# Attention in another order of units: heads two units later, turns behind the heads, a maximum for each map, and four unread products in the second layer

## The reference

```python
def diff_attend(q, k, v, lam):
    s = jnp.einsum('bqhmd,bkhmd->bhmqk', q, k).astype(jnp.float32) * (DA_QK ** -0.5)
    p = jax.nn.softmax(s, axis=-1)
    a = p[:, :, 0] - lam * p[:, :, 1]
    return jnp.einsum('bhqk,bkhv->bqhv', a.astype(v.dtype), v)

def mla_attend(q_nope, q_rope, k_nope, k_rope, v):
    s = (jnp.einsum('bqhd,bkhd->bhqk', q_nope, k_nope)
         + jnp.einsum('bqhr,bkr->bhqk', q_rope, k_rope)).astype(jnp.float32) * MLA_SCALE
    p = jax.nn.softmax(s, axis=-1)
    return jnp.einsum('bhqk,bkhv->bqhv', p.astype(v.dtype), v)
...
        mix = jnp.concatenate([o_da, o_ssd, o_mla], axis=-1) @ w_out[i]
```

## Time and profile before

| | us |
|---|---|
| median of 3 runs | 1402.33 (1400.86, 1402.33, 1531.8) |
| the profiled execution | 1399.01 |
| its span | 1397.2 |
| PE busy | 1146.6 (82%) |
| DVE busy | 429.3 (31%) |
| ACT busy | 299.0 (21%) |
| mean granted clock of PE | 0.90 |

### The profile page before, as it was taken

How to read it: one execution, slowest core, us unless ns; L and a number is a source line. 1 busy time by engine, 2 the same in 40 slices (tenths; PEclk the granted TensorE clock), 3 DMA queues, 4 the chain that set the end, 5 groups by cost and what they waited for, 6 DMA issues and landing times.

```text
span 1397.2 us, 15832 instructions
## 1 busy us (share of the span) xinstructions
PE 1146.6 (82%) x6020; PEld 541.8 (39%) x6020; DVE 429.3 (31%) x997; ACT 299.0 (21%) x694; POOL 64.3 (5%) x71
## 2 busy tenths in 40 slices
PE   4899979978789599999983599988779599995553
PEld 2363423544444333333331447533347233332222
DVE  5111345675622601111110511347662511110003
ACT  2220013425510411111110412013351311110002
POOL 2000021100000200000001000011000100000001
PEclk9999989986999799999997699999789799997776
DMA  9622103939960599999999311307603789999972
GB/s 341 247 80 102 61 0 149 393 132 367 345 258 24 212 336 376 394 394 388 400 401 394 119 59 63 118 5 291 249 0 128 290 319 383 392 413 412 407 315 94
DMA packets 86997, 344.03 MB, mean 246 GB/s; under 512 B 6918, under 2 KB 42187, under 8 KB 64395
## 3 DMA queue, kind: packets, MB, share of 16 engines
q1 hardware_dynamic: 67728, 309.68, 57.5%
q10 hardware_dynamic: 15195, 19.86, 4.2%
q0 software_dynamic: 4000, 13.49, 2.7%
HBM read 300.92 MB, written 42.07 MB: 245 GB/s over the span
## 4 chain that ended last, share of the span: by engine, by line
PE 63%; DMA 19%; DVE 9%; ACT 4%; issue 2%; SPq 1%; POOL 1%; ACTq 0%; POOLq 0%; DVEq 0%
PE ps L933 13%; PE ps L533 12%; DMA ring<-in_exp_w_up 10%; PE ps L956 6%; PE ps L823 6%; PE ps L542 5%; PE ps L476 4%; PE ps L498 3%; DMA slots<-arena 2%; DMA ring<-in_w_mod 2%; PE ps L802 2%; DMA arena<-in_exp_w_up 2%; PE ps L705 2%; PE ps L721 2%; PE ps L782 1%
## 5 line engine op out<-in xcount | busy, mean ns | idle before, releaser
L933 PE MATMUL ps<-ring,arena 128*32 128x256 f32 (+1 forms) x1344 | 196.6, 532 | 45.3 <-DMA ring<-in_exp_w_up 45.3
L533 PE MATMUL ps<-u,ring 128*128 128x512 f32 (+1 forms) x416 | 168.3, 565 | 9.5 <-ACT u L1757 4.0
L476 PE MATMUL ps<-cst,arena 128*128 128x128 f32 (+1 forms) x534 | 107.0, 323 | 68.3 <-DVE arena L1457 33.1
L933 PEld LDWEIGHTS ps<-ring,arena 128*32 128x32 f32 (+1 forms) x1344 | 71.1, 136 | 153.6 <-issue 145.7
L476 PEld LDWEIGHTS ps<-cst,arena 128*128 128x128 f32 (+1 forms) x534 | 67.1, 160 | 161.1 <-issue 74.8
L1613 DVE TENSOR_TENSOR arena<-arena,ps 128x128 f32<-128x128 f32 (+1 forms) x59 | 27.2, 503 | 318.1 <-ACT arena L1940 318.1
L533 PEld LDWEIGHTS ps<-u,ring 128*128 128x128 f32 x416 | 80.0, 194 | 95.2 <-issue 88.1
L933 PE MATMUL ps<-arena 128*64 128x512 f32 (+1 forms) x544 | 82.8, 533 | 17.7 <-DMA arena<-in_exp_w_up 17.7
L956 PE MATMUL ps<-arena 128*32 128x256 f32 (+1 forms) x672 | 94.3, 485 | 1.6 <-ACT arena L1949 1.6
L823 PE MATMUL ps<-u,ring 128*128 128x512 f32 (+1 forms) x256 | 83.6, 487 | 4.3 <-DVE u L1405 3.1
L1940 ACT ACTIVATE arena<-ps 128x256 f32<-128x256 f32 (+1 forms) x44 | 15.3, 348 | 329.8 <-PE ps L933 302.0
(11 more groups left out here) (292 smaller groups left out, 1097.6 us busy)
## 6 DMA issues: line engine op xcount, KB each, us to landing
ring<-in_w_mod SPq DMA_DIRECT2D x24, 2048.0 KB, 10.0
ring<-in_exp_w_gate SPq DMA_DIRECT2D x22, 2048.0 KB, 18.1
ring<-in_exp_w_up SPq DMA_DIRECT2D x22, 2048.0 KB, 22.5
arena<-in_exp_w_down SPq DMA_DIRECT2D x22, 2048.0 KB, 18.0
slots<-zeros SPq DMA_DIRECT2D x4, 6144.0 KB, 41.0
arena<-in_exp_w_gate SPq DMA_DIRECT2D x10, 2048.0 KB, 19.4
u<-in_exp_w_down SPq DMA_DIRECT2D x10, 2048.0 KB, 19.4
arena<-in_exp_w_up SPq DMA_DIRECT2D x10, 2048.0 KB, 24.8
```

Source lines behind the costliest of these rows:

```text
L476: return nc.tensor.transpose(dst, src, ident[0:n, 0:n])
L533: last = nc.tensor.matmul(bank[row:row + width, 0:T - c0], w[:, k, n:n + width], u[:, k, c0:T], start=(k == 0), stop=(k == KT - 1))
L933: last = nc.tensor.matmul(ps[n * part:n * part + n, 2 + b % 2, 0:2 * width].rearrange("p (s n) -> p s n", s=2), x_k, pair[:, :, a:a + widt ...
```

## The change

Six things are changed, all in attention and at its end.

1. PE's order within a step is now: scores of unit s, the modulation part, the heads, and only then the turn of unit s-3. The heads now lag by 5 (units s-7 and s-5), and all steps of the norm and the placing by 2 more than before, so that each layer's loop is 2 steps longer.
2. ACT computes the exponentials of unit s before it copies the turned probabilities of unit s-3.
3. The maximum of a da unit is two instructions, one for each map, each with a signal of its own, and the exponential of a map waits for its own maximum.
4. The output projection runs over k = 2 to 7, then 0 and 1. Before its first product it waits for the ml heads, and before its first k = 0 for the da heads. The banks of the heads are chosen so that its first group lies in the bank of the ml heads.
5. In the second layer PE multiplies the identity with 512 columns of `qk` (128x128x512) into bank 7 behind the scores of units 0, 1, 2 and 3. Nothing reads the result.
6. `maps_through` counts the maxima for the waits.

```diff
-LAG_TURN, LAG_PV, LAG_SQUARE, LAG_MEAN, LAG_ROOT, LAG_ML, LAG_DA = 3, 3, 10, 10, 11, 11, 12
+WARM_UNITS = 4
+LAG_TURN, LAG_PV, LAG_SQUARE, LAG_MEAN, LAG_ROOT, LAG_ML, LAG_DA = 3, 5, 12, 12, 13, 13, 14
...
+def maps_through(s):
+    return 3 * (s // 2) + (3 if s % 2 else 2)
...
-        def heads_of(kind):
-            return ps[:, 0 if kind == "da" else 1, 0:256]
+        ml_bank = {}
+        def heads_of(l, kind):
+            return ps[:, 1 - ml_bank[l] if kind == "da" else ml_bank[l], 0:256]
...
-                    n = s - LAG_TURN
-                    if 0 <= n < len(units):
-                        kind, t, hh, nk = units[n]
-                        pe.wait_ge(S("mixed"), before + n + 1)
...
+                    ml_bank[l] = len(entry) % 2
                     if s < len(units):
                         kind, t, hh, nk = units[s]
...
                         last.then_inc(S("scores_done"), 1)
+                    if l == 1 and s < WARM_UNITS:
+                        nc.tensor.matmul(ps[:, MOD_BANK, :], ident, qk[:, 2, :], start=True, stop=True)
                     spare(mod_in_attention(l, s))
                     n = s - LAG_PV
...
                         last.then_inc(S("heads_done"), 1)
+                    n = s - LAG_TURN
+                    if 0 <= n < len(units):
+                        kind, t, hh, nk = units[n]
+                        pe.wait_ge(S("mixed"), before + n + 1)
...
+                        for k in range(nk // P):
+                            last = tr(turned_probs(n, nk)[:, P * k:P * k + P], probs_of(n)[:, 0, P * k:P * k + P])
+                        last.then_inc(S("probs_turned"), 1)
...
-                        for k in range(KT):
+                        for k in (2, 3, 4, 5, 6, 7, 0, 1):
+                            if n == m == 0 and k in (2, 0):
+                                pe.wait_ge(S("heads_placed"), placed_count(l, last_tile, "da" if k == 0 else "ml"))
...
-                        v.tensor_reduce(nb[:, s, 0:nm], scores_of(kind)[:, :, 0:nk], AX.X, ALU.max,
-                                        negate=True).then_inc(S("max_ready"), 1)
+                        for m in range(nm):
+                            v.tensor_reduce(nb[:, s, m:m + 1], scores_of(kind)[:, m, 0:nk], AX.X, ALU.max,
+                                            negate=True).then_inc(S("max_ready"), 1)
...
+                    if s < len(units):
+                        kind, t, hh, nk = units[s]
+                        if s >= 4:
+                            act.wait_ge(S("probs_turned"), units0 * l + s - 3)
+                        for m in range(2 if kind == "da" else 1):
+                            act.wait_ge(S("max_ready"), 3 * units0 // 2 * l + (maps_through(s - 1) if s else 0) + m + 1)
+                            last = a(probs_of(s)[:, m, 0:nk], scores_of(kind)[:, m, 0:nk], ACT.Exp,
+                                     bias=nb[:, s, m:m + 1], accum_out=rs[:, s, m:m + 1])
+                        last.then_inc(S("exp_done"), 1)
                     n = s - LAG_TURN
                     if 0 <= n < len(units):
                         nk = units[n][3]
...
```

More of the change, by code:

```diff
@@ L801, in attention @@
                                 r, c = 64 * (hh % 2), P * (hh // 2)
-                                last = nc.tensor.matmul(heads_of(kind)[r:r + 64, c:c + P],
+                                last = nc.tensor.matmul(heads_of(l, kind)[r:r + 64, c:c + P],
                                                         v[:, k, 64 * hh:64 * hh + 64], probs_t[:, unit % 4, k, :],
@@ L806, in attention @@
                         last.then_inc(S("heads_done"), 1)
+                    n = s - LAG_TURN
+                    if 0 <= n < len(units):
+                        kind, t, hh, nk = units[n]
+                        pe.wait_ge(S("mixed"), before + n + 1)
+                        if n >= 1 and units[n - 1][3] == NCTX:
+                            pe.wait_ge(S("probs_t_ready"), before + n)
+                            if nk > NCTX:
+                                pe.wait_ge(S("mod_placed"), MODS_FIRST // 5)
+                        elif n >= 2:
+                            pe.wait_ge(S("probs_t_ready"), before + n - 1)
+                        for k in range(nk // P):
+                            last = tr(turned_probs(n, nk)[:, P * k:P * k + P], probs_of(n)[:, 0, P * k:P * k + P])
+                        last.then_inc(S("probs_turned"), 1)
                     i = tile_part(l, s, LAG_MEAN)
@@ L815, in out_projection @@
                 c0 = P * FIRST_T[l]
-                pe.wait_ge(S("heads_placed"), placed_count(l, len(attention_units(l)) // HEAD_UNITS - 1, "da"))
+                last_tile = len(attention_units(l)) // HEAD_UNITS - 1
                 for n in range(2):
@@ L821, in out_projection @@
                         bank = open_bank(name)
-                        for k in range(KT):
+                        for k in (2, 3, 4, 5, 6, 7, 0, 1):
+                            if n == m == 0 and k in (2, 0):
+                                pe.wait_ge(S("heads_placed"), placed_count(l, last_tile, "da" if k == 0 else "ml"))
                             last = nc.tensor.matmul(bank[:, 0:T - c0], w[:, k, P * m:P * m + P], u[:, k, c0:T],
-                                                    start=(k == 0), stop=(k == KT - 1))
+                                                    start=(k == 2), stop=(k == 1))
                         close_bank(last)
@@ L1401, in place_heads @@
                 t, tiles_back = FIRST_T[l] + i, units0 // HEAD_UNITS * l
-                heads = heads_of(kind).rearrange("p (m n) -> p m n", n=P)
+                heads = heads_of(l, kind).rearrange("p (m n) -> p m n", n=P)
                 if kind == "da":
@@ L1860, in attention @@
                             act.wait_ge(S("o_means"), tiles_back + i)
-                        a(o_sq, heads_of("da"), ACT.Square).then_inc(S("o_squared"), 1)
+                        a(o_sq, heads_of(l, "da"), ACT.Square).then_inc(S("o_squared"), 1)
                     i = tile_part(l, s, LAG_ROOT)
@@ L1878, in attention @@
                             S("probs_t_ready"), 1)
[L1879 to L1887, removed]
             def experts(l):
```

## The result

| | before | after |
|---|---|---|
| median us | 1401.59 (4 runs) | 1357.94 (4 runs) |
| ratio | | 0.9695, 95% interval 0.9666 to 0.9724 |
| span of the profiled execution | 1397.2 | 1354.0 |
| mean granted clock | 0.90 | 0.921 |

The forecast was 1364 in a range of 1357 to 1386. One of the four runs before took 1531.8 us and is left out of the ratio. The kernel is 43.2 us shorter by its spans, where the sum had 35.0. The median after of 1357.94 us lies at the lower end of the range; the profiled execution, from which the rows of the changed kernel come, took 1355.8.

The account below looks back on a forecast made before the run. The order of waits in attention, not PE or DVE, bounds the kernel, and clock falls add to it. Gains of 22.4 us in the first layer and 12.6 in the second, together 35.0, take 1399.0 to 1364.0; range 1357 to 1386.

Parts of the forecast that it names:

- the stall: Attention: PE's heads wait for ACT's copy of an older unit, behind the newest exponentials; lag 5 removes this wait.
- The full pair: Pair of units over 512 keys: 4.7 us, between bounds 4.1 and 5.9, allowing a few tenths for PSUM hand-overs.
- The split maximum: DVE, 24 da units: 0.06 us more each, 1.4 in all; first exponential some 0.55 us sooner, held in the 4.7.
- The small units: First layer, six pairs over 256 keys: 3.2 us each, 19.2 in all, gain 6.4, no clock fall expected.
- the 3 us bound: First layer, 256-key units: most that turns waiting for the previous unit's copy cost, 3.7 for 3.2 over six pairs.
- The products: Second layer's start: first two free, last two bring the clock back early; gain 4.4 us, or 0.5 if late.
- The tail: Last scores to output projection, each layer: 7.5 us of PE work, never idle, against 10.65 before; gain 3.1.
- The end of attention is on the path: Behind attention: the output projection follows at once and nothing with a fixed time eats the gain.
- rival F: Behind attention: expert weights arriving at a fixed time eat the first layer's gain; 1386 us, chance 5%.
- The rival E: Full units, both layers: clock falls and stays at 1.2 GHz, pairs take 8.2 us; 1434 in all, chance 4%.
- The signs: Timelines: pairs of 4.4 to 5.0 us, no idle released by ACT's copy, DVE over 80% busy, clock 1.00, tail 7.5.
- the two signs that would make the prediction wrong: PE in attention: the clock falls in full units, or a wait on DVE's mix or a copy precedes turns.

Follow-up runs that it names:

- early placing: Changed kernel with DVE placing finished heads ahead of the maximum of the same step; 1356.8 us.
- The last kernel above: Changed kernel with DVE placing heads ahead of the maximum, and ACT's copy ahead of the exponentials in the first layer's 256-key units only; 1354.44 us, ratio 0.9681.

## Why the prediction was right

**The stall and its removal.** The prediction put the loss on the heads that wait for ACT's copy behind the newest exponentials. In the changed kernel no heads wait for that copy, and at lag 4 they do again, 10.1 us in all, in a kernel 14.5 us longer. That the lag removes the stall is shown. What lag 5 would give in the kernel before, with nothing else changed, was not run.

**The full pair was mis-sized.** 4.7 us was taken, "near the low end"; it measured 3.96 to 4.41, with one of 5.52. The three stages with full pairs beat their forecast by 6.5 us. Eleven pairs, 4.28 on average, make 4.6 of it, and the pieces at the two ends, from the last da scores to the end of the ml scores, the other 1.9: they were taken at 3.6 and took 2.65. The allowance for hand-overs in one PSUM place was the error: in the steady stretches PE was busy without a gap. The split maximum and the later turn are part of why, since without either the second layer's pairs take 4.4 and 4.6. The best pair seen before (4.11) would have been the better term.

**The small units** came out as costed (19.1 for 19.2), with no fall of the clock. The agreement is in part luck. The wait of the turn on the copy, costed at nothing, stood there with 0.17 to 0.88 us at a time, and DVE's list did not hide all of it: with the copy first and early placing the six pairs take 1.5 us less than with early placing alone, half of the 3 us bound. The idle before the fall at 318.5, which the prediction put among those of 1.5 us or more, was 1.31 us in the trace.

**The products.** Forecast: those behind 0 and 1 free, the clock falling behind them all the same and back after the third or fourth, scores 6 at 4.4 us less. Measured: free, falling in the 3.05 us of idle, back near 976.5, 4.9 us less. The stretch without them is 4.5 us longer. The bounds were 0.5 and 4.4, and the upper one held, a little exceeded. The reason given was that two dense products lie close together; one does it as well.

**The split maximum.** Its cost was right (0.06 us). Its gain was put into the pair without a number; it is 7.7 us, of which 0.9 stand in the second layer's last four pairs and a part comes through the clock.

**The tail** was mis-sized the other way: 8.5 us, not 7.5. In the changed kernel's tail PE waits for the placing of the da heads and for a copy:

```profile
1001.97 1.09 PE L800 MATMUL ps<-arena 128*64 128x128 f32 x16 [1.25 <-DVE u L1419]
...
1006.03 0.63 PE L484 MATMUL ps<-cst,arena 128*128 128x128 f32 x4 [0.33 <-ACT arena L1899]
```

That is 1.6 us where the prediction had PE "never without work". The list itself took 6.9 us, less than the 7.5 counted. That placing is a wait that I had looked at on DVE's side only (0.4 us of work) and not as something PE's heads queue behind.

**The end of attention is on the path.** Nothing behind it ate the gain: rival F falls.

**The rival E**, a clock that falls because PE's work is scores and turns and stays down through the full units, came in no kernel. With the turn alone in its old place the clock was at 0.59 over the small units and down for the first two full pairs, but there PE had long idle pieces of 0.6 to 2.6 us, which is not E's reason.

**The signs.** No heads wait for ACT's copy, no L836 record waits for the da heads, DVE is busy for 86 to 93% of the steady stretches, and the clock is at 1.00 from 305 to 372 and from 977 on, as was said. Full pairs are quicker than the 4.4 to 5.0 named, and the tail is 8.5 and not 7.5. One of the two signs that would make the prediction wrong did come: waits on a copy and, once, on DVE's mix stand before PE's turns (rows 312.98 and 334.00). By its own words, then, the prediction is wrong on that point. The sign was too strict: the stage with most of these waits took 19.1 us for 19.2, and taking them away with the copy first was worth 1.5.

## What to carry to other kernels

Where three engines pass units around, the lag of each step is part of the schedule: a step should wait only for what was issued a whole step earlier, and an older unit's copy should never stand between the newest unit's maximum and its next scores. Change such orders together: PE's turn moved back alone cost 39 us here, and 13 us together with ACT's copy. And an unread product that is there for the clock is worth its time only if no stall follows that lets the clock fall again. Look at the clock first when a small edit costs much: with the copy first 6.9 of 7.9 us stood in four pairs behind a fall.

## What the runs showed of the hardware that I had not expected

- PE ran at 1.2 GHz for 17 us with hardly a gap of idle (975 to 992 without the products), doing scores over 32 and 96 rows and transposes, and at the end heads of 64 columns. In eleven of the twelve kernels that had a product of 128 rows and 512 columns behind unit 2, the changed one among them, the rise followed 2.6 to 3.4 us after its start; in the one with a single maximum over both maps it took 5.9 us. Why that one differs stays open.
- With the copy first the clock fell at 323.7 though no idle piece just before it was over 0.5 us; the two falls that the prediction read came behind 1.31 us of idle and within 2.23. The last kernel above ran the same order over the same units with no fall. In PE's rows just before, it lacks one wait of 0.33 us, for the placing of the da heads; whether that decides was not tested.
- Two maxima over 512 columns follow each other at 0.60 us though each is recorded with 0.69.
